# Two transformer blocks on one core: the order of work in attention steps 18 to 24 and of the low parts in the first chunk

## The reference

```python
q_a, k_a, q_i, k_i, q_d, k_d = rope(...)          # of proj = rmsnorm(x) @ w_in
o_a = dsa_attention(q_a, k_a, v_a, q_i, k_i, w_i)  # 8 heads of 64, keys chosen by top-k
o_d = (softmax(q1 k1^T) - lam * softmax(q2 k2^T)) v_d   # 4 heads, causal
o_d = rmsnorm(o_d, g_diff_sub) * (1 - lam_init)
x = x + rmsnorm(concat(o_a, o_d) @ w_out, g_post_mix)
x = x + rmsnorm(relu(rmsnorm(x) @ w_up)^2 @ w_down)
```

## Time and profile before

| what | value |
|---|---|
| median of 3 runs | 1122.55 us (1122.26 to 1122.75) |
| the profiled execution | 1122.77 us, its span 1120.9 us |
| busy: PE, PEld, DVE, ACT, POOL | 99%, 84%, 63%, 36%, 61% |
| granted TensorE clock | 0.999 of full speed |
| HBM read, written | 105.09 MB, 4.19 MB |
| attention steps 18 to 24 | about 695 to 720 us from the span's start |

### The profile page before, as it was taken

How to read it: one execution, slowest core, us unless ns; L and a number is a source line. 1 busy time by engine, 2 the same in 40 slices (tenths; PEclk the granted TensorE clock), 3 DMA queues, 4 the chain that set the end, 5 groups by cost and what they waited for, 6 DMA issues and landing times.

```text
span 1120.9 us, 17285 instructions
## 1 busy us (share of the span) xinstructions
PE 1110.6 (99%) x6175; PEld 942.2 (84%) x6175; DVE 704.9 (63%) x1381; ACT 402.0 (36%) x817; POOL 682.7 (61%) x460
## 2 busy tenths in 40 slices
PE   9999999999999999999999999999999999999997
PEld 7888888998889998888778777677899888999886
DVE  5999778850158853547789777666887113885023
ACT  5146566530015631120202346645665000554012
POOL 7879946586636686667456433135847763568662
PEclk9999999999999999999999999999999999999999
DMA  7421222342213343334343231112224832235412
GB/s 252 132 89 62 75 80 90 113 132 94 94 60 111 114 150 96 105 99 132 113 126 100 84 86 58 38 58 75 76 76 136 184 94 65 90 110 181 158 57 75
DMA packets 52251, 115.54 MB, mean 103 GB/s; under 512 B 21840, under 2 KB 22480, under 8 KB 52176
## 3 DMA queue, kind: packets, MB, share of 16 engines
q1 hardware_dynamic: 31200, 105.40, 29.0%
q10 hardware_dynamic: 20976, 9.15, 3.4%
HBM read 105.09 MB, written 4.19 MB: 97 GB/s over the span
## 4 chain that ended last, share of the span: by engine, by line
PE 97%; ACT 2%; DVE 1%; DMA 0%; issue 0%; SPq 0%; ACTq 0%; DVEq 0%
PE bank L750 21%; PE bank L751 21%; PE bank L752 21%; PE bank L1428 5%; PE bank L1427 5%; PE bank L1426 5%; PE bank L782 2%; PE bank L784 2%; PE bank L783 2%; PE bank L1261 2%; PE bank L1275 1%; PE bank L823 1%; PE bank L833 1%; PE bank L824 1%; PE bank L1303 1%; PE bank L1215 1%
## 5 line engine op out<-in xcount | busy, mean ns | idle before, releaser
L552 POOL TENSOR_TENSOR wl<-raw,wh 128x1024 fp32r<-128x1024 f32 x140 | 337.3, 2409 | 11.7
L549 POOL TENSOR_SCALAR wh<-raw 128x1024 fp32r<-128x1024 f32 x139 | 148.9, 1072 | 257.9 <-PE bank L752 143.2
L750 PE MATMUL bank<-xh,wh 128*128 128x512 f32 (+2 forms) x672 | 234.5, 349 | 0.0
L752 PE MATMUL bank<-xh,wl 128*128 128x512 f32 (+2 forms) x672 | 229.4, 341 | 0.0
L751 PE MATMUL bank<-xl,wh 128*128 128x512 f32 (+2 forms) x672 | 229.1, 341 | 0.0
L750 PEld LDWEIGHTS bank<-xh,wh 128*128 128x128 f32 x672 | 126.8, 189 | 29.0 <-issue 16.4
L1660 ACT ACTIVATE wh<-bank 128x512 fp32r<-128x512 f32 x96 | 52.2, 597 | 253.1 <-DVE bank L2335 109.6
L752 PEld LDWEIGHTS bank<-xh,wl 128*128 128x128 f32 x672 | 126.8, 189 | 14.2
L751 PEld LDWEIGHTS bank<-xl,wh 128*128 128x128 f32 x672 | 126.9, 189 | 12.7 <-issue 0.2
L750 PE MATMUL bank<-uh,wh 128*128 128x512 f32 x288 | 112.8, 392 | 0.0
L752 PE MATMUL bank<-uh,wl 128*128 128x512 f32 x288 | 112.1, 389 | 0.0
(11 more groups left out here) (378 smaller groups left out, 2286.6 us busy)
## 6 DMA issues: line engine op xcount, KB each, us to landing
raw<-wstream SPq DMA_DIRECT2D x188, 512.0 KB, 3.5
x<-xT SPq DMA_DIRECT2D x8, 256.0 KB, 5.1
x4rows<-x_rows ACTq DMA_DIRECT2D x4, 512.0 KB, 9.0
out<-x4rows SPq DMA_DIRECT2D x8, 256.0 KB, 2.1
qd<-ropey ACTq DMA_DIRECT2D x16, 64.0 KB, 2.1
kd<-ropey ACTq DMA_DIRECT2D x16, 64.0 KB, 2.1
qa<-ropey SPq DMA_DIRECT2D x16, 64.0 KB, 2.0
ka<-ropey SPq DMA_DIRECT2D x16, 64.0 KB, 2.0
```

The lines of the kernel that those rows point to most:

```text
L549: nc.gpsimd.tensor_scalar(wh[c][:], raw[c][:], 1.0, 1.0, ALU.mult, ALU.mult).then_inc(high_ready, 1)
L552: nc.gpsimd.tensor_tensor(wl[c][:], raw[c][:], wh[c][:].bitcast(F32), ALU.subtract).then_inc(split_ready, 1)
L750: mm(out, wh_, mh, start=start, stop=False)
L752: return mm(out, wl_, mh, start=False, stop=stop)
```

## The change

On PE, the spreads of heads 2 and 3 (steps 19 and 20) go behind `values`. On ACT, `head_roots(17)` goes from the end of step 17 into step 18, behind `keep_turned(18)` and in front of `exp(20)`. On DVE, `shift(21)` goes in front of `head_factors(1)` in step 19, and `rope_odd(9)` goes from the end of step 19 into step 20, behind `normalise(20)` and in front of the low part of head 2. `PIECES` gives step 21 one piece in place of two and step 24 three in place of two. In the first chunk, the low matmul of tiles 4 to 6 goes behind the two high ones of the next tile. No instruction is added or removed.

```diff
--- before.py
+++ after.py
@@ -101,8 +101,7 @@
 
 SPREAD_AT = {14: 0, 15: 1, 19: 2, 20: 3}
 HIGH_AT = {16: 0, 17: 1, 19: 2, 20: 3}
-LOW_AT = {20: 2, 21: 3}
-PIECES = {19: 1, 20: 1, 21: 2, 24: 2, 27: 2, 30: 2, 31: 2, 32: 2}
+PIECES = {19: 1, 20: 1, 21: 1, 27: 2, 30: 2, 31: 2, 32: 2}
 OUT2_BANKS = (0, 6, 2, 3)
 X1_BANKS = (4, 5, 6, 3)
 QK_BANKS = (0, 1, 2, 0, 1, 2, 0, 2)
@@ -933,7 +932,7 @@
 
             def first_chunk():
 
-                for k in range(KT):
+                def of_high(k):
                     ks = slice(k * P, k * P + P)
                     if k == 6:
                         pe.wait_ge(split_ready, 1)
@@ -942,8 +941,19 @@
                     pe.wait_ge(xh_ready, k + 1)
                     mm(bank[0][:], wh[0][:, ks], xh[:, k], start=k == 0, stop=False)
                     mm(bank[0][:], wl[0][:, ks], xh[:, k], start=False, stop=False)
+
+                def of_low(k):
                     pe.wait_ge(xl_ready, k + 1)
-                    last = mm(bank[0][:], wh[0][:, ks], xl[:, k], start=False, stop=k == KT - 1)
+                    return mm(bank[0][:], wh[0][:, k * P:k * P + P], xl[:, k], start=False, stop=k == KT - 1)
+
+                for k in range(4):
+                    of_high(k)
+                    of_low(k)
+                of_high(4)
+                for k in range(4, KT):
+                    if k < KT - 1:
+                        of_high(k + 1)
+                    last = of_low(k)
                 last.then_inc(chunk_done, 1)
 
             def chunk_highs_first(c, between=None):
@@ -1353,14 +1363,14 @@
                     out2_piece(piece)
                 if 0 <= n < TILES:
                     turn(n)
+                if n >= 1:
+                    values(n - 1)
                 if n in SPREAD_AT and SPREAD_AT[n] == 2:
                     pe.wait_ge(bc_used, 10)
                     norm_spread(10)
                 if n in SPREAD_AT and SPREAD_AT[n] == 3:
                     pe.wait_ge(xl_ready, 3 * KT + 3)
                     norm_spread(11)
-                if n >= 1:
-                    values(n - 1)
                 if n in (5, 9):
                     head_sums(n // 4 - 1)
                 if n in (16, 17):
@@ -1841,15 +1851,19 @@
                 act.wait_ge(sums_done, n // 8 * 2 + 7)
                 A(sd[:, 0:8], NB[:, 0:8], ACT.Sqrt).then_inc(sd_ready, 1)
 
+            def head_high(h):
+
+                act.wait_ge(chunk_done, C_OUT2)
+                act.wait_ge(bc_used, 9 + h)
+                A(xh[:, 4 + h], kept[h][:] if h < 2 else NB[:], ACT.Copy).then_inc(xh_ready, 1)
+
             def step(n):
                 if 0 <= n < TILES:
                     keep_turned(n)
+                if n == 18:
+                    head_roots(17)
                 if n in HIGH_AT:
-
-                    h = HIGH_AT[n]
-                    act.wait_ge(chunk_done, C_OUT2)
-                    act.wait_ge(bc_used, 9 + h)
-                    A(xh[:, 4 + h], kept[h][:] if h < 2 else NB[:], ACT.Copy).then_inc(xh_ready, 1)
+                    head_high(HIGH_AT[n])
                 ends_head = n % 4 == 0 and 1 <= n // 4 <= DIFF_HEADS
                 if n == DIFF_TILES:
                     keep_output(DIFF_HEADS - 1)
@@ -1865,8 +1879,8 @@
                         A(ym[:, o], bank[(2, 7)[o % 2]][:], ACT.Copy).then_inc(evacuated, 1)
                 if ends_head and n < DIFF_TILES:
                     keep_output(n // 4 - 1)
-                if n in (9, 17):
-                    head_roots(n)
+                if n == 9:
+                    head_roots(9)
                 if n > DIFF_TILES + TB and n % TB == 1 or n == TILES:
 
                     pair = (n - DIFF_TILES - 1) // TB - (n != TILES)
@@ -2677,17 +2691,23 @@
                 dve.wait_ge(bc_done, 8 + 2 * b)
                 V.reciprocal(rn[:, 0:8], sd[:, 0:8]).then_inc(rn_ready, 2)
 
+            def head_low(h):
+
+                if h == 2:
+                    dve.wait_ge(xl_ready, 3 * KT + 2)
+                    lows[0] += 2
+                dve.wait_ge(xh_ready, lows[0] + 1)
+                V.tensor_tensor(xl[:, 4 + h], NB[:], xh[:, 4 + h].bitcast(F32), ALU.subtract).then_inc(xl_ready, 1)
+                lows[0] += 1
+
             def step(n):
                 if 0 <= n < TILES:
                     normalise(n)
-                if n in LOW_AT:
-                    h = LOW_AT[n]
-                    if h == 2:
-                        dve.wait_ge(xl_ready, 3 * KT + 2)
-                        lows[0] += 2
-                    dve.wait_ge(xh_ready, lows[0] + 1)
-                    V.tensor_tensor(xl[:, 4 + h], NB[:], xh[:, 4 + h].bitcast(F32), ALU.subtract).then_inc(xl_ready, 1)
-                    lows[0] += 1
+                if n == 20:
+                    rope_odd(9, E_QK + 6)
+                    head_low(2)
+                if n == 21:
+                    head_low(3)
                 if n in (4, 8):
                     top_max()
                 if n in (-1, 5, 9):
@@ -2698,10 +2718,10 @@
                     qk_second(9)
                 if n == 18:
                     rope_even(9)
+                if n + 2 < TILES:
+                    shift(n + 2)
                 if n == 19:
                     head_factors(1)
-                if n + 2 < TILES:
-                    shift(n + 2)
                 if n == 12:
                     head_factors(0)
                 if n in SPREAD_AT:
@@ -2733,8 +2753,6 @@
                     qk_second({2: 6, 6: 7, 10: 8}[n])
                 if n in (3, 7, 11):
                     qk_join({3: 6, 7: 7, 11: 8}[n])
-                if n == 19:
-                    rope_odd(9, E_QK + 6)
             for k in range(KT // 2):
                 x3_scale(k)
             low_of(3, bank[1][:])
```

## The result

The changed kernel takes 1125.22 us (median of 9 runs, 1123.77 to 1126.0), the kernel before beside it 1122.65 (1122.26 to 1122.96): 2.6 us more, a ratio of 1.0023 with a 95% interval of 1.0015 to 1.0032. The forecast was 1123.7, the range ended at 1124.6. The runs also lie further apart, 2.2 us where before had 0.7. The profiled execution took 1125.79 us, its span 1124.1.

A forecast was written before the change was run, and what follows sets the result against it. PE, busy 99% of the span, was taken as the bound, with late transfers holding scores(24). Delay +0.55, moved piece +0.69 and first chunk -0.1 gave +1.15 on 1122.55: 1123.7 us, range 1122.4 to 1124.6.

The forecast's parts named there:

- The copies: ACT, step 18: copies in front of the root let turn(19) follow its piece without a wait, 0.67 less on PE.
- the shift: DVE, step 19: shift(21) in front of the reciprocal fills the wait for the root, at no cost.
- the spread of head 2: PE, step 19: behind values(18) it hides the reciprocal; the norm's product follows 0.2 later than before.
- the rotated sum: DVE, step 20: behind the division of tile 20 it ends 1.0 later, bounds 0.8 and 1.4.
- the rival of the dearer switch: ACT: the root's table load waits or costs 1.28 more, the sum ends 1.1 later than forecast; 1124.8 us, chance 8%.
- The spread of head 3: PE, step 20: behind values(19), it brings scores(23) 0.9 before their old start.
- the arrival at scores(24): PE, step 22: with one piece less in step 21, PE stands before scores(24) at 706.7.
- The landing: SP's eight transfers land 1.0 later, at 708.8; PE waits some 2.1 us and scores(24) start 0.55 later.
- The piece: The piece moved out of step 21 is done behind the wait before scores(24), adding 0.69 at PE's rate.
- The first chunk: PE, first chunk: lows behind the next highs fill waits for x, gaining 0.06 to 0.17, taken as -0.1.
- the three rivals: Transfers do not hold PE (1121.5 us, 7%); the sum is no later (1122.65, 8%); the root's switch gets dearer (1124.8, 8%).
- the one on the slow side: The rival that the root's table load on ACT gets dearer and delays the sum: 1124.8 us, chance 8%.

The follow-up runs named there:

- e1: The changed kernel with the last rotated sum back at the end of DVE's step 19: 1122.83 us against 1122.77 before, ratio 1.0001.
- e8: The kernel before with one edit, the rotated sum in step 20 behind the division: 1122.92 us against 1122.32 before, ratio 1.0003.
- e3: The changed kernel with two filler matmuls on constants in front of scores(24): 1124.15 us against 1122.77 before, ratio 1.0014.
- e7: The changed kernel with one filler matmul in front of scores(24): 1123.82 us against 1122.32 before, ratio 1.0012.
- e10: The changed kernel with one half-width filler matmul (256 columns) in front of scores(24): 1124.37 us against 1122.63 before, ratio 1.0018.
- e2: The changed kernel with two pieces in step 21 and two in step 24, as before: 1123.12 us against 1122.77 before, ratio 1.0006.
- e9: The changed kernel itself measured once more, nothing altered: 1125.63 us against 1122.63 before, ratio 1.0026.

## Why the prediction was wrong

**The copies, the shift, the spread of head 2, the rotated sum:** right. Behind scores(20), turn(19) was put at 3.04 and came at 3.05. The sum was put 1.0 later and SP's first issue came 1.04 later (7.67 for 6.63). The table load ran 1.28 with the root right behind it, so the rival of the dearer switch fell, with its 1124.8.

**The spread of head 3 and the arrival at scores(24):** right, scores(23) forecast at 9.11 and measured at 9.07. A wait of 2.1 was forecast and was 2.11, but that agreement is luck: both of its ends came 0.25 late. On the near side scores(23) took 0.3 longer than before (1.43 for 1.13), since DVE's shift(22) reads their second bank until 703.78 + 0.55 = 704.33, so PE stood before scores(24) 12.1 behind scores(20) and not 11.9. The forecast had taken the old length over. It cost nothing, because the landing came later still.

**The landing:** the mechanism was right, its term was short by 0.25, +0.55 for a measured +0.80. The sum gave 0.04 of it. The rest is the way from SP's first issue to scores(24), which took 6.64 where I had set 6.43 (e1: 6.43, e8: 6.42). The longest time from issue to landing was 2.0 before and 2.2 in the changed kernel. Why it grew is open.

**The piece:** right. +0.69 expected. In e1, e3, e7 and e10 the norm's sums are later by that and by the delay of scores(24), to within 0.1; in e2 and e8, where the piece is in its old place, by the delay alone.

**The first chunk:** right. The next chunk started 0.39 behind the last low part of x, where it was 0.47 (row of before at 9.72 and 13.41 in the earlier trace rows): 0.08 against the 0.1 taken. The other profiles with this edit show 0.38 to 0.40, apart from that of e7 (1.44). There the matmuls of the first chunk stood 0.43 us apart until 10.66, past the point where the others had gone over to 0.23, and the second chunk started 0.9 later than in e3. So an execution can also be longer by what happens in its first microseconds, which the stretch behind scores(20) leaves out.

```profile
9.99 3.23 DVE L2016 SCALAR_TENSOR_TENSOR xl<-x,cols,xh 128x512 fp32r<-128x512 f32 x4 [0.51 <-ACT xh L1511]
...
13.61 0.40 PE L969 MATMUL bank<-xh,wh 128*128 128x512 f32 x1
```

**The step that failed** is "Behind that point there is one piece more to do than before, ... at PE's rate". PE's rate was taken for given on both sides of a wait that I had myself put at 2.1 us, when no row of before had an idle of that length in front of matmuls (the longest wait in its view of waits is 1.5). It fell to half for 3.4 us and cost 1.5. The term was put at nothing without a reason. Without that term the sum is 0.80 + 0.69 - 0.08 = 1.41, which is what e3 and e7 measured as medians (+1.38, +1.50), at 1124.1 inside the range. With it, it is 2.9 in an execution with the fall, and between the two as a median. None of the three rivals held it: the one on the slow side put the loss on ACT's table load.

## What to carry to other kernels

Before an instruction is moved behind another, follow what it feeds to the end, through the queue of transfers too: here 6.4 us of transfers hung on one sum, with 0.5 to spare, and the two waits that the change removed were worth nothing while those transfers set the next start. A long wait on the matmul engine can cost more than its length, here at 2.1 us in most executions: price the matmuls behind it at the half clock as well, and if it can't be removed, fill it. When a hand-written order has several engines this close, removing a wait mostly uncovers the next one, so measure the stretch between two fixed events and not the wait.

## What the runs showed of the hardware

The granted TensorE clock fell to its lower level, 1.2 GHz, behind an idle of 2.11 and 2.12 us (changed kernel, e9), which followed transposes, values and scores. It did not fall in the idle but 0.8 and 1.5 us after the scores had begun again, and it was back at 2.4 GHz some 3.4 us later (from about 710.1 to 713.5, and from 710.4 to 713.8). Matmuls of 512 columns took 0.43 in place of 0.23. With an idle of 0.8, 0.9, 1.0 or 1.4 us at the same place (e2, e1, e7, e10) it stayed at 2.4 GHz in each profile. By its times the changed program falls in most executions and not in all, which I take to be why its runs spread over 2 us; both of its profiles show the fall. What decides in a given execution is open. That the length of the idle alone decides is not shown either, as the fillers of e7 and e10 also add matmuls in front of it.
